# A transformer block on one core: weight slots at new SBUF distances, and another output stage

## The chip, the cores and the metric

The kernel runs on one NeuronCore of one Trainium2 chip. The metric is the device time of one execution in microseconds (us); several executions of the same program give a median. A profile is one more execution, recorded engine by engine.

The engines are named as the profile names them: PE is TensorE's matmul stream and PEld its stream of weight loads, DVE is VectorE, ACT is ScalarE, POOL is GpSimd, SP is the queue that mostly issues transfers. SBUF is the on-chip memory in front of the engines; an address in this text is a byte offset inside each of its 128 partitions. PSUM is the accumulator memory, in eight banks of 128 x 512 float32.

## What is computed

One trunk layer on x of 512 tokens x 2048 channels, float32. Cut to what matters:

```python
h = rmsnorm(x, norm_mix_pre)
y = hybrid_mixer(h, w_in, ...)          # 16 heads of forgetting attention, and an RG-LRU branch
x = x + rmsnorm(y, norm_mix_post)
h = rmsnorm(x, norm_ffn_pre)
g = causal_dwconv(h @ w_gate, conv_ffn_w, conv_ffn_b)
y = (gelu(g) * (h @ w_up)) @ w_down     # D_FF = 6144
x = x + rmsnorm(y, norm_ffn_post)       # the output
```

## The kernel before, in words

**Layout and precision.** The host lays everything out channel-major: a tile is 128 channels x 512 tokens, and there are KT = 16 tiles of x. The weights lie in DRAM in the order of use, in units of 128 x 1024 numbers (4096 bytes in each partition, eight 128 x 128 blocks of 512 bytes). Every number that enters a matmul is split into a high part (rounded by an ACT copy) and a low part (the DVE difference), and `product()` (L1475) makes three matmuls out of one: high x high, high x low, low x high. The first operand is the stationary one, loaded by a weight load, the second the moving one, streamed through. A unit is therefore 24 matmuls. SP brings a unit into `raw`, ACT writes its high half into a weight slot, DVE the low half, PE uses the slot.

**Weight slots.** Slots 0 and 1 are `w_hi[:, 0]`, `w_lo[:, 0]` and `w_hi[:, 1]`, `w_lo[:, 1]` (L143, L144). The fast products below use a third slot as well, `w_hi2`, `w_lo2` (L231, L232); `w_slot(q)` (L324) hands out slot 2, 0, 1 in turn.

**Stages.** In order of time:
1. the mixer: projections, attention, recurrence and the output projection, with the weight unit stationary (128 x 128) and the activations `act_hi`, `act_lo` moving, 512 columns wide;
2. the first six hidden tiles of gate and up (PLAIN), in the same form;
3. the other NS = 42 hidden tiles by a scheme with seven instead of eight products (L1700): `fast_product(i, n, ...)`, n from 0 to 6, each 24 matmuls with a stationary weight block and 256 moving columns of `act_hi`, `act_lo` (n = 0, 4, 5) or of the sums `tsum` (n = 1, 2, 3, 6). Product q = 7i + n uses slot 2 where q is a multiple of 3, then slot 0, then slot 1. The hidden tiles go to DRAM (`h_spill`) and come back;
4. the down projection (L1739): four groups of 24 units; here the activations are stationary and a weight slot (0 or 1) moves, 512 columns;
5. the end.

**The end.** The down projection leaves its result token-major: `y_tile(i)` for i = 0 to 3 holds 128 tokens x 2048 channels, three quarters of it in SBUF, the last quarter still in banks 4 to 7. `last_unit` (L1749) finishes one bank after the other. For each i (ACT L855, DVE L1457): ACT squares the bank (L834), DVE adds the four partial sums (L1459), ACT takes the root (L861), DVE inverts it (L1461), ACT scales the last quarter (L864) while DVE scales the first three (L1463). Then PE transposes tile after tile back to channel-major (L1785), four 128 x 128 transposes to a tile, into banks 0 to 3 in turn, in the order LIFTS. Twelve tiles (4 to 15) are finished by DVE: gain times tile plus the residual, which POOL has brought back into `x1_b` (L496, 3 MB); SP stores them in pairs (L397). Tiles 0 to 3 are finished by ACT into `y_out` (L871), and POOL sends each with a transfer that adds to what lies in the output (L499); from the third on ACT waits until the transfer before last has landed (`y_added`).

**What sets the order.** Each engine runs its own program in written order; semaphores join them. Nothing is scheduled by a planner.

**Where things lie.** Tensors are allocated in the order of the text, each start rounded up to 32 bytes. From the start of `w_hi` to the start of `act_hi` there are w_hi 8192, w_lo 8192, ones 512, eps 32, rms 2048, sq 4096, acc 2048, ident 512, cols 32, eps_y 32, y_sq 64 and y_r 64 bytes, together 25824, which is 224 modulo 512. `act_lo`, `tsum` and all their 128-column pieces lie at the same place modulo 512 as `act_hi`, and all blocks of a slot at the same place as its start. `w_hi2` lies a multiple of 512 from `act_hi`. So, modulo 512, slots 0 and 1 start 224 bytes below the activations (288 above), slot 2 at the same place. Of the small products in the mixer, `gw` against `xc`, `v` against `pt`, and `q` against `k` all lie at the same place modulo 512.

Of the kernel before, what the change touches and what calls it, by code (L numbers as in the profile page):

```python
# [24 lines left out]
F32R = mybir.dt.float32r  # L25
# [4 lines left out]
P = 128  # L30
# [28 lines left out]
ADDED = 4  # L59
LIFTS = (4, 5, 0, 6, 7, 1, 8, 9, 2, 10, 11, 3, 12, 13, 14, 15)  # L60
# [28 lines left out]
OPEN = 8  # L89
LOG1P = [1.0 / n for n in (15, 13, 11, 9, 7, 5, 3)]  # L90
# [35 lines left out]
def block_kernel(nc, xT, par_d, weights, gate_w, out):  # L126
# [3 lines left out]
    with ExitStack() as ctx:  # L130
# [6 lines left out]
        def sem(name):  # L137
# [8 lines left out]
        eps = sb("eps", [1])  # L146
# [5 lines left out]
        cols = sb("cols", [2, QT])  # L152
        eps_y = sb("eps_y", [QT])
        y_sq = sb("y_sq", [QT, GROUPS])
        y_r = sb("y_r", [3, QT])
# [3 lines left out]
        LIFT = banks[0:4]  # L159
# [71 lines left out]
        w_hi2 = sb_in(ffn, "w_hi2", [UW], F32R)  # L231
        w_lo2 = sb_in(ffn, "w_lo2", [UW], F32R)  # L232
# [10 lines left out]
        y_out = sb_in(hid, "y_out", [2, S])  # L243
        hid.close()
        fin = ExitStack()
        x1_b = sb_in(fin, "x1_b", [KT - ADDED, S])
# [16 lines left out]
            x1_back_landed lifted added taken  # L263
# [16 lines left out]
         eps_y_done, x1_back_landed, lifted, added, taken,  # L280
# [4 lines left out]
        y_added = [sem(f"y_added{s}") for s in range(2)]  # L285
# [38 lines left out]
        def w_slot(q):  # L324

            k = (q + 2) % 3
            return (w_hi2[:], w_lo2[:]) if k == 2 else (w_hi[:, k], w_lo[:, k])
# [8 lines left out]
        def _(sp):  # L336
# [168 lines left out]
        def _(act):  # L505
            def split(u, s):

                act.wait_ge(raw_landed[s], (u - s) * 8 + 16)
                at_least(act, unit_used, u - 1)
                act.activation(w_hi[:, s], raw[:, s], ACT.Copy).then_inc(hi_done, 1)  # L510

            def split_down(n, s):
# [3 lines left out]
                act.activation(w_hi[:, s], raw[:, s], ACT.Copy).then_inc(hi_done, 1)  # L516
# [310 lines left out]
            def down_square(g, i):  # L827
# [6 lines left out]
                act.activation(sq[:, 0], src, ACT.Square, accum_out=y_sq[:, i, g:g + 1]).then_inc(wdsq_done, 1)  # L834

            for g in range(GROUPS):
# [19 lines left out]
                if g < GROUPS - 1:  # L856
                    both(n + PER_GROUP, 0, 0)
            for i in range(QT):
                down_square(GROUPS - 1, i)
                act.wait_ge(y_summed, i + 1)  # L860
                act.activation(y_r[:, 1, i:i + 1], y_r[:, 0, i:i + 1], ACT.Sqrt, scale=1.0 / D,  # L861
                               bias=eps_y[:, i:i + 1]).then_inc(y_std_done, 1)
                act.wait_ge(y_r_done, i + 1)
                act.activation(y_tile(i)[:, 3 * S:], DOWN_BANKS[1][i][:], ACT.Copy, scale=y_r[:, 2, i:i + 1]).then_inc(  # L864
                    y_scaled_a, 1)
            for n, k in enumerate(LIFTS):
                if k < ADDED:
                    act.wait_ge(lifted, n + 1)
                    if k > 1:
# [977 lines left out]
```

## Time and profile before

| | us |
|---|---|
| median of 3 executions | 2336.46 (2334.82 to 2336.62) |
| the profiled execution, its own time | 2338.33 |
| span of its profile | 2336.7 |
| PE busy in it | 2281.6 (98%) |
| DVE, ACT, POOL busy | 1540.5, 996.5, 192.3 |
| granted TensorE clock, mean | 0.99 |

The span is what the trace covers; the profiled execution took 1.6 us more, and 1.9 us more than the median. In the chain of waits that ended last PE holds 94%; DVE has 2%, ACT, DMA and issue 1% each. A matmul's record is longer than its share of the time, since matmuls overlap: what one costs is the distance from its start to the next one's.

### The profile page before, as it was taken

To read this page: it belongs to the slowest core of one execution; us is meant where nothing else is said; L and a number is where in the kernel's file an instruction comes from. 1 tells how busy PE (TensorE), PEld (TensorE's weight loads), DVE (VectorE), ACT (ScalarE), POOL (GpSimd) and SP (SyncE) were. 2 spreads that over 40 slices of the span, in tenths; PEclk is the share of its full clock that TensorE was granted. 3 is DMA by queue.
4 is the path that set the end of the run, shared out by engine and by line. 5 is a ranking of instruction groups with operands and counts; after the bars stand their busy time and mean duration, and the time that the engine had idled before them with its cause. 6 is when DMAs were issued, how large, how long until landed. Compare 5 with 4: busy or idle time off the path is not lost.

```text
span 2336.7 us, 34768 instructions
## 1 busy us (share of the span) xinstructions
PE 2281.6 (98%) x13392; PEld 1998.7 (86%) x13392; DVE 1540.5 (66%) x1999; ACT 996.5 (43%) x1259; POOL 192.3 (8%) x239
## 2 busy tenths in 40 slices
PE   7999999999899899999999999999999999999996
PEld 5788888888688688999999999999998888888885
DVE  8676667667754677777777777777775444444443
ACT  5444444444422354444444444444443333343433
POOL 3000000003300000111111111111112000000000
PEclk9899999999999999999999999999999999999998
DMA  4222222222242335777777777777767332222423
GB/s 167 74 85 83 83 92 81 92 83 81 90 136 91 114 123 168 207 199 194 197 195 198 200 197 196 202 197 200 202 187 269 127 99 90 97 92 93 150 90 99
DMA packets 94246, 328.31 MB, mean 141 GB/s; under 512 B 10672, under 2 KB 14896, under 8 KB 93888
## 3 DMA queue, kind: packets, MB, share of 16 engines
q1 hardware_dynamic: 69024, 240.33, 30.0%
q0 software_dynamic: 22816, 82.36, 16.3%
q10 hardware_dynamic: 2304, 4.20, 0.5%
q8 instruction: 73, 1.20, 0.2%
q14 instruction: 29, 0.24, 0.0%
HBM read 305.83 MB, written 21.00 MB: 140 GB/s over the span
## 4 chain that ended last, share of the span: by engine, by line
PE 94%; DVE 2%; ACT 1%; issue 1%; DMA 1%; SPq 0%; POOL 0%; DVEq 0%; POOLq 0%; ACTq 0%
PE bank L1478 31%; PE bank L1479 31%; PE bank L1480 31%; PE bank L1540 1%; DVE acc_b L1142 0%; DMA x_sb<-xT 0%; ACT act_hi L636 0%; DMA out<-y_out 0%; DVE w_lo L882 0%; PE bank L1785 0%; PE bank L1508 0%; DMA h_t<-h_spill 0%; ACT w_hi L510 0%; PE bank L1559 0%; ACT act_hi L660 0%
## 5 line engine op out<-in xcount | busy, mean ns | idle before, releaser
L1478 PE MATMUL bank<-act_hi,w_hi 128*128 128x512 f32 (+1 forms) x2112 | 729.1, 345 | 22.8 <-DVE act_lo L897 14.9
L1479 PE MATMUL bank<-act_lo,w_hi 128*128 128x512 f32 (+1 forms) x2112 | 723.9, 343 | 0.0
L1480 PE MATMUL bank<-act_hi,w_lo 128*128 128x512 f32 (+1 forms) x2112 | 722.7, 342 | 0.0
L1478 PEld LDWEIGHTS bank<-act_hi,w_hi 128*128 128x128 f32 x2112 | 400.4, 190 | 80.0 <-issue 15.6
L1480 PEld LDWEIGHTS bank<-act_hi,w_lo 128*128 128x128 f32 x2112 | 400.3, 190 | 51.0
L1479 PEld LDWEIGHTS bank<-act_lo,w_hi 128*128 128x128 f32 x2112 | 400.3, 190 | 48.6 <-issue 0.5
L1479 PE MATMUL bank<-tsum,w_hi 128*128 128x256 f32 x1344 | 378.5, 282 | 0.0
L1478 PE MATMUL bank<-tsum,w_hi 128*128 128x256 f32 x1344 | 378.1, 281 | 0.0
L1480 PE MATMUL bank<-tsum,w_lo 128*128 128x256 f32 x1344 | 377.7, 281 | 0.0
L892 DVE TENSOR_TENSOR w_lo<-raw,w_hi 128x1024 fp32r<-128x1024 f32 x96 | 117.5, 1224 | 296.5 <-ACT w_hi L516 296.5
L1478 PE MATMUL bank<-w_hi,act_hi 128*128 128x512 f32 x768 | 303.5, 395 | 0.8 <-DVE w_lo L892 0.8
L1479 PE MATMUL bank<-w_lo,act_hi 128*128 128x512 f32 x768 | 303.4, 395 | 0.0
L1480 PE MATMUL bank<-w_hi,act_lo 128*128 128x512 f32 x768 | 303.4, 395 | 0.0
L882 DVE TENSOR_TENSOR w_lo<-raw,w_hi 128x1024 fp32r<-128x1024 f32 x138 | 171.9, 1245 | 197.5 <-ACT w_hi L510 194.5
L797 ACT ACTIVATE w_hi<-raw_s 128x1024 fp32r<-128x1024 f32 x168 | 178.6, 1063 | 251.3 <-PE bank L1480 248.9
L1348 DVE TENSOR_TENSOR w_lo<-raw_s,w_hi 128x1024 fp32r<-128x1024 f32 x168 | 205.8, 1225 | 82.1 <-ACT w_hi L797 82.1
L1480 PEld LDWEIGHTS bank<-tsum,w_lo 128*128 128x128 f32 x1344 | 254.4, 189 | 0.0
L1478 PEld LDWEIGHTS bank<-tsum,w_hi 128*128 128x128 f32 x1344 | 254.4, 189 | 0.0
L1479 PEld LDWEIGHTS bank<-tsum,w_hi 128*128 128x128 f32 x1344 | 254.2, 189 | 0.0
L510 ACT ACTIVATE w_hi<-raw 128x1024 fp32r<-128x1024 f32 x138 | 145.9, 1057 | 254.0 <-PE bank L1480 254.0
L516 ACT ACTIVATE w_hi<-raw 128x1024 fp32r<-128x1024 f32 x96 | 101.7, 1060 | 305.9 <-PE bank L1480 295.1
L1478 PEld LDWEIGHTS bank<-w_hi,act_hi 128*128 128x128 f32 x768 | 144.0, 187 | 36.2 <-DVE w_lo L892 1.0
(236 smaller groups left out, 2509.3 us busy)
## 6 DMA issues: line engine op xcount, KB each, us to landing
raw<-weights SPq DMA_DIRECT2D x318, 512.0 KB, 3.5
raw_s<-weights SPq DMA_DIRECT2D x84, 512.0 KB, 4.6
raw_s<-weights POOLq DMA_DIRECT2D x84, 512.0 KB, 6.1
raw_a<-weights SPq DMA_DIRECT2D x42, 512.0 KB, 4.0
h_spill<-h_out POOLq DMA_DIRECT2D x48, 256.0 KB, 3.6
h_t<-h_spill POOLq DMA_DIRECT2D x24, 512.0 KB, 6.6
x<-xT POOLq DMA_DIRECT2D x16, 256.0 KB, 3.0
out<-x ACTq DMA_DIRECT2D x16, 256.0 KB, 2.1
```

What stands on the lines that cost most here:

```text
L510: act.activation(w_hi[:, s], raw[:, s], ACT.Copy).then_inc(hi_done, 1)
L516: act.activation(w_hi[:, s], raw[:, s], ACT.Copy).then_inc(hi_done, 1)
L797: act.activation(w_slot(q)[0], RAW_OF[n](i), ACT.Copy).then_inc(hi_done, 1)
L882: dve.tensor_tensor(w_lo[:, s], raw[:, s], word(w_hi[:, s]), ALU.subtract).then_inc(split_done, 1)
L892: dve.tensor_tensor(w_lo[:, s], raw[:, s], word(w_hi[:, s]), ALU.subtract).then_inc(split_done, 1)
L1348: dve.tensor_tensor(lo, RAW_OF[n](i), word(hi), ALU.subtract).then_inc(split_done, 1)
L1478: pe.matmul(dst, ah, bh, start=start, stop=False, skip_group_check=goes_on)
L1479: pe.matmul(dst, ah, bl, start=False, stop=False, skip_group_check=goes_on)
L1480: return pe.matmul(dst, al, bh, start=False, stop=stop, skip_group_check=goes_on)
L1540: last = pe.transpose(PT[b][:, bc + P * (qt - j):bc + P * (qt - j) + P], sm[:, c:c + P], ident[:])
```

## The change

**Weight slots.** `w_0`, `w_1` and `w_2` hold high and low half of a slot one behind the other. Fillers of 64 bytes (`line_of_0`, `line_of_1`, `line_of_2`) and a new order of the tensors set where they start. Modulo 512 slot 0 now starts 64 bytes below the activations, slot 1 128 bytes below, slot 2 64 bytes above. The stream of matmuls keeps its number, order and shapes up to the last product.

**The end.** The squares are scaled by 1/D in the ACT instruction; the three earlier partial sums and the epsilon are added up by DVE before the last unit ends (`y_p`), so that the root needs only its own square. ACT takes a root of a constant ahead of them. ACT scales the last quarter of token tile i-1 after the square of tile i. All 16 channel tiles are finished by DVE in `x1_b` (now 16 tiles, read back as 4 MB, two down units later) and stored by SP one by one; `y_out`, `added`, `y_added` and POOL's adding transfers are gone. PE transposes into eight banks, and the first four channel tiles of token tiles 0 to 2 ahead of the fourth token tile.

```diff
-ADDED = 4
-LIFTS = (4, 5, 0, 6, 7, 1, 8, 9, 2, 10, 11, 3, 12, 13, 14, 15)
+LINE = 64
...
         par = sb("par", [NPAR])
+        eps = sb("eps", [1])
+        cols = sb("cols", [2, QT])
+        eps_y = sb("eps_y", [QT])
+
+        w_1 = sb("w_1", [2, UW], F32R)
+        sb("line_of_1", [LINE // 4])
+        w_0 = sb("w_0", [2, UW], F32R)
         raw = sb("raw", [2, UW])
-        w_hi = sb("w_hi", [2, UW], F32R)
-        w_lo = sb("w_lo", [2, UW], F32R)
         ones = sb("ones", [P])
...
         ident = sb("ident", [P])
+        sb("line_of_0", [LINE // 4])
+        w_hi, w_lo = (w_0[:, 0], w_1[:, 0]), (w_0[:, 1], w_1[:, 1])
...
-        w_hi2 = sb_in(ffn, "w_hi2", [UW], F32R)
-        w_lo2 = sb_in(ffn, "w_lo2", [UW], F32R)
+        sb_in(ffn, "line_of_2", [LINE // 4])
+        w_2 = sb_in(ffn, "w_2", [2, UW], F32R)
...
-            for k in range(0, KT - ADDED, 2):
-                sp.wait_ge(taken, k + 2)
-                sp.dma_start(out[:, ADDED + k:ADDED + k + 2], x1_b[:, k:k + 2]).then_inc(stored, 16)
-            sp.wait_ge(stored, 16 * (KT - ADDED) // 2)
+            for k in range(KT):
+                sp.wait_ge(taken, k + 1)
+                sp.dma_start(out[:, k], x1_b[:, k]).then_inc(stored, 16)
+            sp.wait_ge(stored, 16 * KT)
...
-            pool.wait_ge(h_split, 3 * PER_GROUP + 6)
-            pool.dma_start(x1_b[:], out[:, ADDED:KT]).then_inc(x1_back_landed, 16)
-            for k in range(ADDED):
-                pool.wait_ge(added, k + 1)
-                pool.dma_start(out[:, k], y_out[:, k % 2], accum_op=ALU.add).then_inc(y_added[k % 2], 16)
-            for e in range(2):
-                pool.wait_ge(y_added[e], 16 * ADDED // 2)
+            pool.wait_ge(h_split, (GROUPS - 1) * PER_GROUP + KT // 2)
+            pool.dma_start(x1_b[:], out).then_inc(x1_back_landed, 16)
...
+            act.activation(y_s[:, 0:1], eps[:, 0:1], ACT.Sqrt).then_inc(y_std_done, 1)
+            act.wait_ge(y_std_done, 1)
+            act.wait_ge(y_summed, 3)
             for i in range(QT):
                 down_square(GROUPS - 1, i)
+                if i:
+                    scale_last(i - 1)
+                token_root(i)
+            scale_last(QT - 1)
...
+            dve.tensor_tensor(y_p[:, 0], y_sq[:, 0], y_sq[:, 1], ALU.add).then_inc(y_summed, 1)
+            dve.tensor_tensor(y_p[:, 1], y_sq[:, 2], eps_y[:], ALU.add).then_inc(y_summed, 1)
+            dve.wait_ge(y_summed, 2)
+            dve.tensor_tensor(y_p[:, 0], y_p[:, 0], y_p[:, 1], ALU.add).then_inc(y_summed, 1)
...
+            for k in range(KT):
+                dve.wait_ge(lifted, k + 1)
+                dve.scalar_tensor_tensor(out=x1_b[:, k], in0=banks[k % 8][:], scalar=col("g_ffn_post", k),
+                                         in1=x1_b[:, k], op0=ALU.mult, op1=ALU.add).then_inc(taken, 1)
...
+            for i in range(QT - 1):
+                pe.wait_ge(y_scaled_d, i + 1)
+                for k in range(4):
+                    lift(k, i)
+            pe.wait_ge(y_scaled_d, QT)
+            for k in range(4):
+                lift(k, QT - 1).then_inc(lifted, 1)
+            pe.wait_ge(y_scaled_a, QT)
+            for k in range(4, KT):
+                at_least(pe, taken, k - 7)
                 for i in range(QT):
-                    if n == 0:
-                        pe.wait_ge(y_scaled_d, i + 1)
-                    last = pe.transpose(LIFT[n % 4][:, P * i:P * i + P], y_tile(i)[:, P * k:P * k + P], ident[:])
+                    last = lift(k, i)
                 last.then_inc(lifted, 1)
```

How the change moves instructions is shown at two places. The first is ACT's program from the last split of activations on (`sq` the scratch of the squares, `y_r`, `y_s` root and inverse, `y_a`, `y_b` the token tiles). Before:

```order
L524 ACTIVATE act_hi<-h_t 128x4x256 [waits unit_used]
L834 ACTIVATE sq,y_sq<-bank4 128x512 [waits last_done]
L861 ACT_TABLE_LOAD
L861 ACTIVATE y_r<-y_r,eps_y 128x1 [waits y_summed]
L864 ACTIVATE y_a<-bank4,y_r 128x512 [waits y_r_done]
L834 ACTIVATE sq,y_sq<-bank5 128x512 [waits last_done]
L861 ACTIVATE y_r<-y_r,eps_y 128x1 [waits y_summed]
L864 ACTIVATE y_a<-bank5,y_r 128x512 [waits y_r_done]
```

and in the changed kernel:

```order
L522 ACTIVATE act_hi<-h_t 128x4x256 [waits unit_used]
L868 ACT_TABLE_LOAD
L868 ACTIVATE y_s<-eps 128x1
L832 ACTIVATE sq,y_sq<-bank4 128x512 [waits last_done,y_summed,y_std_done]
L865 ACTIVATE y_s<-y_sq,y_p 128x1 [waits wdsq_done]
L832 ACTIVATE sq,y_sq<-bank5 128x512 [waits last_done]
L859 ACTIVATE y_a<-bank4,y_r 128x512 [waits y_r_done]
L865 ACTIVATE y_s<-y_sq,y_p 128x1 [waits wdsq_done]
L832 ACTIVATE sq,y_sq<-bank6 128x512 [waits last_done]
```

The table load has moved ahead of the first square of the last group, the root waits for ACT's own square only, and each scaling stands behind the next square.

The second is PE's program behind the last product: the transposes. Before, from the first to the one that waits for a freed bank:

```order
L1785 MATMUL bank0<-ident,y_a 128x128 [waits y_scaled_d] x2
L1785 MATMUL bank0<-ident,y_b 128x128 [waits y_scaled_d] x2
L1785 MATMUL bank1<-ident,y_a 128x128 x2
L1785 MATMUL bank1<-ident,y_b 128x128 x2
L1785 MATMUL bank2<-ident,y_a 128x128 x2
L1785 MATMUL bank2<-ident,y_b 128x128 x2
L1785 MATMUL bank3<-ident,y_a 128x128 x2
L1785 MATMUL bank3<-ident,y_b 128x128 x2
L1785 MATMUL bank0<-ident,y_a 128x128 [waits taken]
```

and in the changed kernel, the fourth token tile's and what follows:

```order
L1784 MATMUL bank0<-ident,y_b 128x128 [waits y_scaled_d]
L1784 MATMUL bank1<-ident,y_b 128x128
L1784 MATMUL bank2<-ident,y_b 128x128
L1784 MATMUL bank3<-ident,y_b 128x128
L1784 MATMUL bank4<-ident,y_a 128x128 [waits y_scaled_a]
L1784 MATMUL bank4<-ident,y_a 128x128
L1784 MATMUL bank4<-ident,y_b 128x128 x2
L1784 MATMUL bank5<-ident,y_a 128x128 x2
L1784 MATMUL bank5<-ident,y_b 128x128 x2
```

Twelve transposes now stand before the first row of this piece, three to each of banks 0 to 3, so that one more completes a tile; the first wait for a freed bank comes with the ninth tile instead of the fifth, and no wait for `added` is left.

## Rows read from the trace of the kernel before

**Rows 1.** The page: span, and section 1 (busy us, share, instructions).
```profile
span 2336.7 us, 34768 instructions
PE 2281.6 (98%) x13392; PEld 1998.7 (86%) x13392; DVE 1540.5 (66%) x1999; ACT 996.5 (43%) x1259; POOL 192.3 (8%) x239
```

**Rows 2.** Groups of PE by form: line, names, shape, xcount | busy us, mean ns | idle before.
```profile
L1478 PE MATMUL bank<-act_hi,w_hi 128*128 128x512 f32 x1104 | 445.6, 404 | 22.8 <-DVE act_lo L897 14.9 <-DVE act_lo L1159 7.0 <-DVE w_lo L882 0.9
L1478 PE MATMUL bank<-tsum,w_hi 128*128 128x256 f32 x1344 | 378.1, 281 | 0.0
L1478 PE MATMUL bank<-w_hi,act_hi 128*128 128x512 f32 x768 | 303.5, 395 | 0.8 <-DVE w_lo L892 0.8
L1478 PE MATMUL bank<-act_hi,w_hi 128*128 128x256 f32 x1008 | 283.5, 281 | 0.0
```

**Rows 3.** Timeline of PE, rounds 18 to 20: start us, us; first matmuls of products 0 and 1.
```profile
1291.22 0.28 PE L1478 MATMUL bank<-act_hi,w_hi 128*128 128x256 f32 x1
...
1294.09 0.28 PE L1478 MATMUL bank<-tsum,w_hi 128*128 128x256 f32 x1
...
1311.17 0.28 PE L1478 MATMUL bank<-act_hi,w_hi 128*128 128x256 f32 x1
...
1314.00 0.28 PE L1478 MATMUL bank<-tsum,w_hi 128*128 128x256 f32 x1
...
1331.08 0.28 PE L1478 MATMUL bank<-act_hi,w_hi 128*128 128x256 f32 x1
...
1333.92 0.28 PE L1478 MATMUL bank<-tsum,w_hi 128*128 128x256 f32 x1
```

**Rows 4.** Timeline of PE, down projection: two matmuls that stand 24 apart.
```profile
2289.97 0.40 PE L1478 MATMUL bank<-w_hi,act_hi 128*128 128x512 f32 x1
...
2295.57 0.40 PE L1478 MATMUL bank<-w_hi,act_hi 128*128 128x512 f32 x1
```

**Rows 5.** Timeline of PE, gate product of the mixer: the first and sixth of six.
```profile
308.92 0.40 PE L1478 MATMUL bank<-xc_hi,gw_hi 128*128 128x512 f32 x1
...
310.06 0.39 PE L1480 MATMUL bank<-xc_hi,gw_lo 128*128 128x512 f32 x1
```

**Rows 6.** Timeline of PE, attention scores: two matmuls that stand two apart.
```profile
364.24 0.40 PE L1479 MATMUL bank<-k_lo,q_hi 64*128 64x512 f32 x1
...
364.71 0.34 PE L1478 MATMUL bank<-k_hi,q_hi 64*128 64x384 f32 x1
```

**Rows 7.** Timeline of the end, ACT and DVE, with the idle time before and its releaser.
```profile
2304.17 0.60 ACT L834 ACTIVATE sq<-bank 128x512 f32<-128x512 f32 x1 [4.93 <-PE bank L1480]
...
2306.17 0.29 ACT L861 ACTIVATE y_r<-y_r,eps_y 128x1 f32<-128x1 f32 x1
...
2312.22 0.29 ACT L861 ACTIVATE y_r<-y_r,eps_y 128x1 f32<-128x1 f32 x1 [0.23 <-DVE y_r L1459]
...
2312.75 1.02 DVE L1463 TENSOR_SCALAR y_b<-y_b,y_r 128x1536 f32<-128x1536 f32 x1
...
2314.40 1.54 DVE L1469 SCALAR_TENSOR_TENSOR x_b<-bank,par,x_b 128x512 f32<-128x512 f32 x2 [0.64 <-PE bank L1785]
...
2316.89 4.29 DVE L1469 SCALAR_TENSOR_TENSOR x_b<-bank,par,x_b 128x512 f32<-128x512 f32 x6 [0.95 <-PE bank L1785]
...
2326.88 0.75 DVE L1469 SCALAR_TENSOR_TENSOR x_b<-bank,par,x_b 128x512 f32<-128x512 f32 x1 [2.00 <-PE bank L1785]
```

**Rows 8.** DMA issues: line, engine, xcount, KB each, us to landing.
```profile
out<-x_b SPq DMA_DIRECT2D x1, 512.0 KB, 5.0
...
out<-x ACTq DMA_DIRECT2D x16, 256.0 KB, 2.1
```

**Rows 9.** SP's queue: the last store.
```profile
2327.66 0.33 SPq L397 DMA_DIRECT2D out<-x_b  x1
```

**Rows 10.** ACT while the residual comes back; one stretch's busy us, PEclk, DMA share, GB/s.
```profile
2213.96 1.06 ACT L516 ACTIVATE w_hi<-raw 128x1024 fp32r<-128x1024 f32 x1 [4.38 <-DMA raw<-weights]
...
2205.00:2210.00 5.00, 5.00 (x23) 4.00 (x22) 1.76 (x3) 2.01 (x2) 0.00 (x0) 1.00 0.98 409
```

More of the change, by code:

```diff
@@ L262, in block_kernel @@
             wd_taken wdsq_done y_summed y_std_done y_r_done y_scaled_a y_scaled_d diag_done spread_done eps_y_done
-            x1_back_landed lifted added taken
+            x1_back_landed lifted taken
             stored dve_chain""".split()
@@ L279, in block_kernel @@
          wd_taken, wdsq_done, y_summed, y_std_done, y_r_done, y_scaled_a, y_scaled_d, diag_done, spread_done,
-         eps_y_done, x1_back_landed, lifted, added, taken,
+         eps_y_done, x1_back_landed, lifted, taken,
          stored, dve_chain) = [sem(n) for n in names]
@@ L857, in _, with scale_last, token_root @@
                     both(n + PER_GROUP, 0, 0)
+            def scale_last(i):
+                act.wait_ge(y_r_done, i + 1)
+                act.activation(y_tile(i)[:, 3 * S:], DOWN_BANKS[1][i][:], ACT.Copy, scale=y_r[:, i:i + 1]).then_inc(
+                    y_scaled_a, 1)
+            def token_root(i):
+                n = QT * (GROUPS - 1) + i + 1
+                act.wait_ge(wdsq_done, n)
+                act.activation(y_s[:, i:i + 1], y_sq[:, GROUPS - 1, i:i + 1], ACT.Sqrt, bias=y_p[:, 0, i:i + 1]).then_inc(
+                    y_std_done, 1)
+            act.activation(y_s[:, 0:1], eps[:, 0:1], ACT.Sqrt).then_inc(y_std_done, 1)
+            act.wait_ge(y_std_done, 1)
+            act.wait_ge(y_summed, 3)
             for i in range(QT):
                 down_square(GROUPS - 1, i)
[L860 to L869, printed above, removed]
[L870 to L872 removed]
+                if i:
+                    scale_last(i - 1)
+                token_root(i)
+            scale_last(QT - 1)
         @block.vector
@@ L1745, in down_unit @@
                         last = product(bank[:], (h_tokens(act_hi, s, kt, i), h_tokens(act_lo, s, kt, i)),
-                                       (w_hi[:, s, w], w_lo[:, s, w]), start and kt == 0, stop and kt == 1)
+                                       (w_hi[s][:, w], w_lo[s][:, w]), start and kt == 0, stop and kt == 1)
                 last.then_inc(unit_used, 1)
@@ L1774, in _, with lift @@
                     last_unit(n + PER_GROUP - 1, 1, out_banks)
-            for n, k in enumerate(LIFTS):
-                if n >= 4:
-                    before = LIFTS[:n - 3]
-                    at_least(pe, taken, sum(b >= ADDED for b in before))
-                    at_least(pe, added, sum(b < ADDED for b in before))
-                if k == 12:
-                    pe.wait_ge(y_scaled_a, QT)
+            def lift(k, i):
+                return pe.transpose(banks[k % 8][:, P * i:P * i + P], y_tile(i)[:, P * k:P * k + P], ident[:])
+            for i in range(QT - 1):
[8 more added lines that the diff above has]
+                at_least(pe, taken, k - 7)
                 for i in range(QT):
-                    if n == 0:
-                        pe.wait_ge(y_scaled_d, i + 1)
-                    last = pe.transpose(LIFT[n % 4][:, P * i:P * i + P], y_tile(i)[:, P * k:P * k + P], ident[:])
+                    last = lift(k, i)
                 last.then_inc(lifted, 1)
```

50 lines of the change are left out of this document (20 added, 30 removed).

## The prediction

> **What bounds the kernel now.** I read the page first: PE is busy for 98% of the span [rows 1]. Only two things can move the time: the distance from one matmul's start to the next, or the end, where PE no longer sets the pace. The groups by form [rows 2] give the counts. There are three times 1104 and three times 768 matmuls of 512 columns, together 5616, and three times 1344 and three times 1008 of 256 columns, together 7056; the latter are 294 products of 24. The idle time before them is about 24 us in all, most of it before the first form. So the timeline is needed for their distances.
>
> *256 columns.* One product 0 stands alone between the tsum products, so its length can be read [rows 3]. It is 1294.09 - 1291.22 = 2.87 us in slot 2, 2.83 in slot 0 (round 19) and 2.84 in slot 1 (round 20). I looked at all 42 rounds: it is the same each time, to 0.01 us. Per matmul that is 119.6, 117.9 and 118.3 ns. Slot 2 is the one that starts at the activations' own place modulo 512 bytes; the other two start 288 above.
>
> *512 columns.* In the down projection 24 matmuls take 5.60 us, 233.3 ns each [rows 4], at slots 0 and 1 alike, and the earlier stages, with the roles of the operands exchanged, run at the same. The small gate product, whose operands lie at the same place modulo 512, has five distances in 1.14 us, 228 ns each [rows 5]. The score product, also at the same place but on 64 partitions, has two in 0.47 us, 235 ns [rows 6]. So the trace shows that the place of a slot can matter, by one or two per cent, and not always in the same direction.
>
> *The end* [rows 7]. From the first square (2304.17) ACT and DVE go in turn: the first root comes at 2306.17, two microseconds later, and three rounds of 2.02 us each follow until 2312.22. DVE scales the last token tile from 2312.75 to 2313.77, the first channel tile is taken from 2314.40, and the last, after gaps, ends at 2327.63. The store issued at 2327.66 [rows 9] takes 5.0 us to land [rows 8], to 2332.66; another 4.0 us end the span.
>
> **The change, part by part.**
>
> *The token rounds.* The first root no longer waits for a table load and DVE's sum: it can start when the square ends, at 2304.17 + 0.69 + 0.02 = 2304.88 (the square of 0.60 and its read of the sum occupied ACT for 0.69). Round 0's DVE scaling starts 0.53 after its root, as at the end before (2312.22 to 2312.75). A round on ACT is now square 0.69, scaling 0.58 and root with handover 0.33, 1.60 us in place of 2.02, since DVE's handovers lie beside the next square. The second square has to wait for its bank, which is ready six matmuls after the first, at 2304.17 + 6 x 0.2333 = 2305.57. The roots then come at 2304.88, 2306.88, 2308.49 and 2310.10. DVE's last scaling runs from 2310.63 to 2311.65, against 2313.77: **2.1 us earlier**. The table load moves into ACT's idle 4.93 us; the three small DVE sums end before the first square too, and if that cover were gone they would cost a few tenths.
>
> *The tiles.* DVE's first tile starts 0.63 after its last scaling, as before, at 2312.28. Six tiles in a row take 4.29 us, 0.715 each; sixteen take 11.44 and end at 2323.72. Before, twelve tiles ended at 2327.63 because DVE stood waiting for banks that ACT held while it waited for its adding transfers. PE has three quarters of four tiles ready and a lead of eight banks, so I cost its transposes at nothing; if the cover went, the next in line is PE's cold clock. **In sum 3.9 us earlier** than before (the 2.1 are in it).
>
> *The stores.* Sixteen of 256 KB in 11.44 us ask for 367 GB/s; with the residual coming back the engines moved 409 [rows 10]. The last store before had 512 KB and an adding transfer beside it and took 5.0; a plain one of 256 KB took 2.1 [rows 8]. I take 2.8, nearer to the latter, because the demand stays below 409. It lands at 2326.6, and 4.0 more give 2330.6: **6.1 us less**, between 3.9 (landing as before) and 6.8.
>
> *The residual* comes back as 4 MB. While 3 MB did, one load of weights came late enough for ACT to wait 4.38 us for it [rows 10], and yet all down units together cost PE 0.8 us of idle [rows 2]. I take nothing; the bound is 2.6 us, the time of the added megabyte at 409 GB/s. POOL's queue holds nothing else behind it.
>
> *Slot 2* moves from distance 0 to 64. Among the 98 products in it each is 0.035 us longer than the mean of the other two slots; if it runs like them, 98 x 0.035 = **3.4 us less**. The other end is nothing, and a gain.
>
> *Slots 0 and 1 at 256 columns* have 196 products. From nothing to the pace of slot 2, 98 x 0.04 + 98 x 0.03 = 6.9 us more. I take nothing: their distances are new, but none of them is 0.
>
> *512 columns.* No row has the new distances of -64 and -128. The bounds are the gate product, 5616 x 5.3 ns = 29.8 us less, and the score product, 5616 x 1.7 ns = 9.5 us more. Slot 0 at -64 is nearest to distance 0, where the two small products disagree in sign; slot 1 at -128 is nearer to the present place. I take nothing, with a chance for the gain below.
>
> The sum is -6.1 - 3.4 = -9.5. The profiled execution would go from 2338.3 to 2328.8, its span to 2327.2; against the median of 2336.46 I forecast **2327.0**.
>
> One rule speaks against the first half of the change. What the rows show is the 2.87 against 2.83 us [rows 3]. The Trainium skill (TensorE: Matmul & The Clock Gate, "Step-by-step: what each phase is for") has PE read its moving operand and its weights through two independent ports, so that loading the next weights takes nothing from the running matmul; by it the slots' places would be worth nothing. This trace disagrees for slot 2, if the place is what sets it apart. The same page ("Back-to-back issue gap") gives N/2.4 + 2.5 ns, as an estimate 216 ns for 512 columns, so that 17 ns of the 233 here would have some other cause; were all of that a clash of two reads and all of it gone, the gain would be near 100 us, which no row supports.
>
> **The rivals.**
>
> *The 512-column matmuls get faster.* For it speaks the gate product at 228 ns [rows 5], in every one of its occurrences; against it the score product. In full the time is 2336.5 - 6.1 - 3.4 - 29.8 = 2297.2. If by nearest row only slot 0's half gains (2808 x 5.3 = 14.9) and its 256-column products pay 3.9, it is 2336.5 - 6.1 - 14.9 + 3.9 = 2319.4.
>
> *The places do nothing.* Slot 2 is longer for another reason than its place, such as its low half lying 4096 bytes behind its high half (8192 in the other slots), and stays so. Then only the end counts: 2336.5 - 6.1 = 2330.4. The rule above says that much too.
>
> *The new places are worse.* Two streams a line apart could meet more often than two far apart; and all three slots now have the 4096 bytes of slot 2. At the pace of slot 2 everywhere and of the score product at 512 columns it costs 6.9 + 9.5 = 16.4, and the time is 2346.8; at half of that, 2338.6. It ends above the present time as soon as the places cost more than the 6.1 us of the end, 1.1 ns for each 512-column matmul or 0.9 ns for each one of 256.
>
> *The transfers bound the end.* Stores one by one run behind DVE and land as late as before, and the fourth megabyte costs PE 1 us: 2336.5 - 3.9 - 3.4 + 1.0 = 2330.2. For it speaks that 367 is close to 409.
>
> **How the numbers follow.** A difference of 0.2% is 4.7 us, about what a measurement of this kernel can tell from no change. My chances are 0.42 for the forecast, 0.25 for faster 512-column matmuls, 0.13 for places that do nothing, 0.12 for worse places and 0.08 for the transfers. The range goes from 2299, which leaves out only the last part of the full gain, to 2338, where worse places cost half; past either end some 2 in 10 stay out. The forecast's own range is 2324 to 2330. Faster by over 0.2%: nearly all of the first (0.41), all of the second (0.25), most of the third and of the last (0.12), 0.78. Slower by over 0.2% takes most of the worse places, 0.11. The rest, 0.11, is within 0.2%.
>
> **What would show it.** In the changed profile product 0 should take 2.83 to 2.84 us in slot 2 as well; 24 matmuls of the down projection should still take 5.60 us, and about 5.47 if the first rival is right; the first root should come 0.7 us after the first square; sixteen tiles should take 11.4 us without a gap on DVE; and the last store should land within 3 us. The forecast is wrong if those 5.60 us change by more than 0.01, either way, since 0.01 us is worth 2.3 us of the kernel, or if DVE waits for PE between tiles.

## The result, and the profile after

The changed kernel takes 2295.27 us (median of 4 executions, 2293.55 to 2299.04) against 2336.54 for the kernel before (4 executions, 2334.82 to 2338.06): a ratio of 0.9826, with a 95% interval of 0.9809 to 0.9843. That is 41 us less, where 9.5 were forecast, and below the end of the range (2299). The profiled execution has a span of 2293.1 us against 2336.7 [rows 1]:

```profile
span 2293.1 us, 34762 instructions
...
PE 2248.9 (98%) x13392; PEld 1975.0 (86%) x13392; DVE 1543.0 (67%) x2002; ACT 993.7 (43%) x1256; POOL 188.5 (8%) x235
```

PE has the same 13392 matmuls and is again busy for 98%, yet its busy time is 33 us shorter. So most of the gain lies in how closely the matmuls follow each other, and the stages show where. In the timeline of PE I take the first matmul of the fast products, the first of the down projection and the last product. Before:

```profile
932.55 0.28 PE L1478 MATMUL bank<-act_hi,w_hi 128*128 128x256 f32 x1
...
1770.46 0.50 PE L1478 MATMUL bank<-w_hi,act_hi 128*128 128x512 f32 x1 [0.84 <-DVE w_lo L892]
...
2307.94 0.40 PE L1480 MATMUL bank<-w_hi,act_lo 128*128 128x512 f32 x1
```

and after:

```profile
925.43 0.28 PE L1485 MATMUL bank<-act_hi,w 128*128 128x256 f32 x1
...
1739.92 0.50 PE L1485 MATMUL bank<-w,act_hi 128*128 128x512 f32 x1 [0.94 <-DVE w L896]
...
2275.98 0.40 PE L1487 MATMUL bank<-w,act_lo 128*128 128x512 f32 x1
```

| us | before | after | gain |
|---|---|---|---|
| up to the first fast product (512 columns, slot stationary) | 932.6 | 925.4 | 7.1 |
| fast products (256 columns) | 837.9 | 814.5 | 23.4 |
| down projection (512 columns, slot moving) | 537.5 | 536.1 | 1.4 |
| from the last product's start to the end of the span | 28.8 | 17.1 | 11.6 |

The four gains are those of one profiled execution on each side and add up to 43.6 us, the difference of the two spans; the medians differ by 41.3. The first stage is the least certain one: another kernel with the same places (the second of the next section) reaches the fast products at 923.1 us, not 925.4.

The rows that answer to those of product 0 [rows 3], rounds 18 to 20, slots 2, 0 and 1:

```profile
1274.02 0.28 PE L1485 MATMUL bank<-act_hi,w 128*128 128x256 f32 x1
...
1276.76 0.28 PE L1485 MATMUL bank<-tsum,w 128*128 128x256 f32 x1
...
1293.36 0.28 PE L1485 MATMUL bank<-act_hi,w 128*128 128x256 f32 x1
...
1296.08 0.28 PE L1485 MATMUL bank<-tsum,w 128*128 128x256 f32 x1
...
1312.68 0.28 PE L1485 MATMUL bank<-act_hi,w 128*128 128x256 f32 x1
...
1315.52 0.28 PE L1485 MATMUL bank<-tsum,w 128*128 128x256 f32 x1
```

Slot 2 (now at +64) takes 2.74 us instead of 2.87, slot 0 (-64) 2.72 instead of 2.83, slot 1 (-128) 2.84 as before.

The end, in the timeline of ACT, DVE and SP, answering to [rows 7]:

```profile
2272.31 0.60 ACT L832 ACTIVATE sq<-bank 128x512 f32<-128x512 f32 x1 [3.49 <-PE bank L1487]
...
2273.03 0.29 ACT L865 ACTIVATE y_s<-y_sq,y_p 128x1 f32<-128x1 f32 x1
...
2277.57 0.29 ACT L865 ACTIVATE y_s<-y_sq,y_p 128x1 f32<-128x1 f32 x1
...
2278.09 1.02 DVE L1471 TENSOR_SCALAR y_b<-y_b,y_r 128x1536 f32<-128x1536 f32 x1
...
2279.60 10.63 DVE L1476 SCALAR_TENSOR_TENSOR x_b<-bank,par,x_b 128x512 f32<-128x512 f32 x16 [0.49 <-PE bank L1784]
...
2280.38 10.21 SPq L400 DMA_DIRECT2D out<-x_b  x16
```

The first root comes 0.72 us after the first square; DVE's last scaling ends 6.8 us after that square (9.6 before); sixteen tiles run without a gap, 0.66 us each; and the last store, issued at 2290.26 and landing 2.5 us later, ends the span but for 0.4 us. In SP's queue the wait behind the last landing has all but gone. Before:

```profile
SPq L130 <- DMA out<-x_b: 4.7, 1, 4.7
SPq L130 <- PEq L130: 3.8, 1, 3.8
```

and after (engine, line, waited for: us in total, times, longest):

```profile
SPq L129 <- DMA out<-x_b: 2.1, 1, 2.1
SPq L129 <- PEq L129: 0.2, 1, 0.2
```

### The profile page after: what moved, and what is told of

The parts are those of the page before. It is cut to its first block, busy times and chain, and to the rows that moved or that the text cites. A ratio compares the mean times of both kernels' runs of the same rounds, so it can differ in the third digit from the quotient of the medians.

```text
span 2293.1 us, 34762 instructions
## 1 busy us (share of the span) xinstructions
PE 2248.9 (98%) x13392; PEld 1975.0 (86%) x13392; DVE 1543.0 (67%) x2002; ACT 993.7 (43%) x1256; POOL 188.5 (8%) x235
## 3 DMA queue, kind: packets, MB, share of 16 engines
q10 hardware_dynamic: 2304, 4.20, 0.5%
## 4 chain that ended last, share of the span: by engine, by line
PE 94%; DVE 3%; issue 1%; ACT 1%; DMA 0%; POOL 0%; SPq 0%; DVEq 0%; POOLq 0%; ACTq 0%
PE bank L1485 31%; PE bank L1486 31%; PE bank L1487 31%; PE bank L1547 1%; DVE x_b L1476 0%; DVE acc_b L1146 0%; DMA x_sb<-xT 0%; DVE act_lo L901 0%; PE bank L1515 0%; DVE w L886 0%; DMA h_t<-h_spill 0%; ACT act_hi L658 0%; ACT w L508 0%; ACT x_sb L642 0%; PE bank L1566 0%
## 5 line engine op out<-in xcount | busy, mean ns | idle before, releaser
L1485 PE MATMUL bank<-act_hi,w 128*128 128x512 f32 (+1 forms) x2112 | 722.4, 342 | 21.5 <-DVE act_lo L901 14.9
L1486 PE MATMUL bank<-act_lo,w 128*128 128x512 f32 (+1 forms) x2112 | 717.5, 340 | 0.0
L1487 PE MATMUL bank<-act_hi,w 128*128 128x512 f32 (+1 forms) x2112 | 717.4, 340 | 0.0
L1485 PEld LDWEIGHTS bank<-act_hi,w 128*128 128x128 f32 x2112 | 398.8, 189 | 76.8 <-issue 16.1
L1487 PEld LDWEIGHTS bank<-act_hi,w 128*128 128x128 f32 x2112 | 398.8, 189 | 47.8
L1486 PEld LDWEIGHTS bank<-act_lo,w 128*128 128x128 f32 x2112 | 398.8, 189 | 46.9 <-issue 0.5
L1486 PE MATMUL bank<-tsum,w 128*128 128x256 f32 x1344 | 374.0, 278 | 0.0
L1485 PE MATMUL bank<-tsum,w 128*128 128x256 f32 x1344 | 373.4, 278 | 0.0
L1487 PE MATMUL bank<-tsum,w 128*128 128x256 f32 x1344 | 373.3, 278 | 0.0
L896 DVE TENSOR_TENSOR w<-raw,w 128x1024 fp32r<-128x1024 f32 x96 | 117.7, 1226 | 295.1 <-ACT w L514 295.0
L1485 PE MATMUL bank<-w,act_hi 128*128 128x512 f32 x768 | 303.0, 395 | 1.0 <-DVE w L896 0.9
L1487 PE MATMUL bank<-w,act_lo 128*128 128x512 f32 x768 | 303.0, 395 | 0.0
L1486 PE MATMUL bank<-w,act_hi 128*128 128x512 f32 x768 | 302.8, 394 | 0.0
L886 DVE TENSOR_TENSOR w<-raw,w 128x1024 fp32r<-128x1024 f32 x138 | 171.9, 1246 | 190.7 <-ACT w L508 188.0
L1487 PEld LDWEIGHTS bank<-tsum,w 128*128 128x128 f32 x1344 | 252.7, 188 | 0.0
L1485 PEld LDWEIGHTS bank<-tsum,w 128*128 128x128 f32 x1344 | 252.6, 188 | 0.0
L508 ACT ACTIVATE w<-raw 128x1024 fp32r<-128x1024 f32 x138 | 145.7, 1057 | 246.6 <-PE bank L1487 241.2
L1486 PEld LDWEIGHTS bank<-tsum,w 128*128 128x128 f32 x1344 | 252.4, 188 | 0.0
L514 ACT ACTIVATE w<-raw 128x1024 fp32r<-128x1024 f32 x96 | 101.7, 1059 | 304.5 <-PE bank L1487 292.6
```

The costliest lines, as they stand in the source:

```text
L508: act.activation(w_hi[s], raw[:, s], ACT.Copy).then_inc(hi_done, 1)
L514: act.activation(w_hi[s], raw[:, s], ACT.Copy).then_inc(hi_done, 1)
L886: dve.tensor_tensor(w_lo[s], raw[:, s], word(w_hi[s]), ALU.subtract).then_inc(split_done, 1)
L896: dve.tensor_tensor(w_lo[s], raw[:, s], word(w_hi[s]), ALU.subtract).then_inc(split_done, 1)
L1485: pe.matmul(dst, ah, bh, start=start, stop=False, skip_group_check=goes_on)
L1486: pe.matmul(dst, ah, bl, start=False, stop=False, skip_group_check=goes_on)
```

## The experiments

Distances below are from the activations to a slot's start, modulo 512 bytes; the change has slots 0, 1 and 2 at -64, -128 and +64, the kernel before at -224, -224 and 0. Where a kernel has one profile and one time only, it is read by its stages: 0.01 us in one product of 24 matmuls is 2.9 us over the 294 fast products.

**The two halves apart.** The first kernel has the new end and the old places, the second the old end and the new places. The diff is the first one's, against the changed kernel.

```diff
-        w_1 = sb("w_1", [2, UW], F32R)
-        sb("line_of_1", [LINE // 4])
-        w_0 = sb("w_0", [2, UW], F32R)
         raw = sb("raw", [2, UW])
+        w_his = sb("w_his", [2, UW], F32R)
+        w_los = sb("w_los", [2, UW], F32R)
...
-        sb("line_of_0", [LINE // 4])
+        sb("as_far_as_before", [56])
...
-        sb_in(ffn, "line_of_2", [LINE // 4])
```

> The changed kernel with the slots where they were before (slots 0 and 1 at -224 from the activations modulo 512 bytes, slot 2 at 0, halves 8192 bytes apart in slots 0 and 1). Theory (the places and the end are two separate gains): the 42 rounds of fast products take 838 us again, as before the change, and from the first square of the last group to the end of the span it takes 20.8 us as in the changed kernel, not 32.5: 2336.5 - 11.7 = 2324.8. Rival (the end was helped by the earlier stages, for instance by transfers that stand otherwise): the end keeps well over 20.8 us.

> The kernel before with the slots at their new places and nothing else. Theory: 2336.5 - 31.9 = 2304.6, of which some 23.4 us in the fast products; product 0 takes 2.72, 2.84 and 2.74 us in slots 0, 1 and 2. Rival (some of it is due to the end's new tensors): less than 28 us of gain.

The end alone: 2327.35 us against 2337.28, ratio 0.9954 (0.9938 to 0.9971). The fast products take 837.8 us as before, and the last product's start stands 17.1 us from the end of the span. The places alone: 2306.36, ratio 0.9868 (0.9852 to 0.9885); fast products 814.5, end 28.6. The gains, 9.9 and 30.9 us, add up to the whole 41.3. So each half works by itself, and neither borrows from the other, as far as these intervals (some 4 us either way) can tell.

**Slot 1 at -64 too.**

```diff
         w_1 = sb("w_1", [2, UW], F32R)
-        sb("line_of_1", [LINE // 4])
         w_0 = sb("w_0", [2, UW], F32R)
```

> The changed kernel with slot 1 too at -64 instead of -128. Theory (what counts is a slot's own distance to the activations): product 0 takes 2.72 us in slot 1 instead of 2.84; 98 products by 0.12 us are 11.8 us, so 2283.5. Rival (the slots have to differ from each other, since ACT and DVE write one while PE reads another): slot 0 loses what it had gained, and the time is 2295 or more.

2277.45 us, ratio to the kernel before 0.9744 (0.9728 to 0.9760): 18 us faster than the change. The timeline of PE, product 0 in slot 0 and in slot 1, then the first down matmul:

```profile
1281.95 0.28 PE L1484 MATMUL bank<-act_hi,w 128*128 128x256 f32 x1
...
1284.67 0.28 PE L1484 MATMUL bank<-tsum,w 128*128 128x256 f32 x1
...
1300.99 0.28 PE L1484 MATMUL bank<-act_hi,w 128*128 128x256 f32 x1
...
1303.71 0.28 PE L1484 MATMUL bank<-tsum,w 128*128 128x256 f32 x1
...
1721.17 0.50 PE L1484 MATMUL bank<-w,act_hi 128*128 128x512 f32 x1 [1.14 <-DVE w L895]
```

All three slots now take 2.72 us, 113.3 ns for a matmul; the 42 rounds take 801.0 us, 13.5 less than in the change; and the stages before them end 5.3 us earlier, at 920.2 (one profile each; the change's places gave 925.4 and 923.1). "Each at its own distance" is thus no help in itself: three slots at the same 64 bytes do better. The 11.8 us I expected left out that slot 2's products drop from 2.74 to 2.72 with a faster neighbour, and the 512-column stages. Slot 1 lies at the same address in this kernel, in the next one and in the whole sweep below; only the activations move against it. Its products take between 2.72 and 2.88 us there, so its own address is not what sets its pace.

**The halves of a slot together, at the old distances.**

```diff
-        sb("line_of_1", [LINE // 4])
...
-        sb("line_of_0", [LINE // 4])
+        sb("line_of_0", [56])
...
-        sb_in(ffn, "line_of_2", [LINE // 4])
```

> The changed kernel with slots 0 and 1 at -224 and slot 2 at 0, as before the change, but with the halves of each slot one behind the other (4096 bytes), as the change has them. Theory (distance to the activations): 2.83, 2.84 and 2.87 us for product 0 in slots 0, 1, 2 as before the change, about 2325. Rival (it is the distance between the halves that counts): slots 0 and 1 change by 0.03 us or more.

2327.31 us (one time), fast products 837.8 us, product 0 at 2.84, 2.84 and 2.86 us. The distance between a slot's halves, which the change altered too, is not the cause.

**A sweep of the distance.** Only the fillers' sizes change: slots 0 and 1 both at one distance, slot 2 at another. In words of four bytes the first filler is 8, 24, 32 and 48 and left out in the last kernel, the second 24, 40, 8, 48 and 16; the diff shows the first of the five.

```diff
-        sb("line_of_1", [LINE // 4])
...
-        sb("line_of_0", [LINE // 4])
+        sb("line_of_0", [8])
...
-        sb_in(ffn, "line_of_2", [LINE // 4])
+        sb_in(ffn, "line_of_2", [24])
```

> The changed kernel with slots 0 and 1 at -32 and slot 2 at +96. Known so far for a 256-column product: 2.72 us at -64 and +64, 2.84 at -128 and -224, 2.87 at 0. Theory (a window around 64 bytes on either side is good, the exact value does not matter): 2.72 to 2.78 us at both. Rival (only whole 64-byte lines are good, 32 and 96 straddle): 2.84 or more at both, 2325 in all.

> The changed kernel with slots 0 and 1 at -96 and slot 2 at +160. Theory (window around 64): -96 between 2.72 and 2.84, +160 at 2.84. Rival (lines): both 2.84.

> The changed kernel with slots 0 and 1 at -128 and slot 2 at +32. Theory (each slot by its own distance): slots 0 and 1 take 2.84 us, so that the 42 rounds take 838 us less what slot 2 gains at +32, and 24 matmuls of the down projection less than 5.60, near 5.57, since slot 1 at -128 must be what made that stage 1.4 us shorter in the changed kernel (slot 0 at -64 shows 5.60 alone). Rival (slots have to differ): the down projection is as before.

> The changed kernel with slots 0 and 1 at -192 and slot 2 at +192. Of the distances so far, those that agree modulo 256 gave the same pace (-96 and +160: 120.0 ns; -224 and +32: 118.3 and 118.1). Theory (256 bytes are the period): -192 and +192 are +64 and -64 modulo 256, 2.72 us for every product and 801 us for the 42 rounds. Rival (512 is the period, only the nearest lines are good): 2.84 or more.

> The changed kernel with slots 0 and 1 at the activations' own place (0), slot 2 at +64. At 256 columns both theories expect 2.86 us in slots 0 and 1. At 512 columns: if the gate product of the mixer (228 ns, operands at the same place) tells what a slot at 0 does, the time up to the first fast product is 918 us or less and 24 matmuls of the down projection take 5.47 us. Rival (a short product of six matmuls does not tell it): 5.60 us and 930 us.

The stages in us, from the same three points of PE's timeline, with those kernels that have slots 0 and 1 at one distance (42 rounds and down projection in us):

| slots 0 and 1 | slot 2 | to the first fast product | product 0 in slot 0 | 42 rounds | down projection | single time |
|---|---|---|---|---|---|---|
| -224 (new end, halves together) | 0 | 933.0 | 2.84 | 837.8 | 537.6 | 2327.31 |
| -192 | +192 | 933.6 | 2.72 | 801.1 | 527.9 | 2280.97 |
| -128 | +32 | 930.0 | 2.84 | 836.6 | 538.1 | 2323.51 |
| -96 | +160 | 931.2 | 2.88 | 847.6 | 541.1 | 2338.57 |
| -64 | +64 | 920.2 | 2.72 | 801.0 | 537.5 | 2277.44 |
| -32 | +96 | 932.6 | 2.80 | 826.3 | 538.5 | 2316.13 |
| 0 | +64 | 913.4 | 2.88 | 842.3 | 522.7 | 2297.24 |

The last row's points in the timeline of PE are:

```profile
913.40 0.28 PE L1483 MATMUL bank<-act_hi,w 128*128 128x256 f32 x1
...
1755.74 0.50 PE L1483 MATMUL bank<-w,act_hi 128*128 128x512 f32 x1 [0.70 <-DVE w L894]
...
2278.43 0.39 PE L1485 MATMUL bank<-w,act_lo 128*128 128x512 f32 x1
```

Three things follow. *At 256 columns* 64 bytes are best, on either side, and so are 192: of the distances tried, those that agree modulo 256 agree in pace (-192 is +64, and -96 is +160), so the period is 256 bytes, not 512. The neighbouring -96 is the slowest of all, 120.0 ns a matmul, slower than anything in the kernel before, so neither the window around 64 of my first theory nor its rival, under which -32 should have been no better than 2.84 us, holds. *At 512 columns* 0 is best by far, and the first rival's row was right: the down projection takes 226.9 ns for a matmul at 0, where the gate product [rows 5] had shown 228; -192 shows 229 and the other distances 233 to 235. *The sign counts there*: a slot at -64 gains where it is stationary (920.2) and not where it moves (537.5); a slot at -192, that is +64, gains where it moves (527.9) and not where it is stationary (933.6). Both say that at 512 columns the stationary block should start at the moving operand's place or 64 bytes below it.

The third kernel's expectation missed on the down projection: -128 alone does not shorten it. That the change's mixture of -64 and -128 does, by 1.4 us, is not explained; in the change's trace the units of slot 1 take 5.58 us on the mean and those of slot 0 5.60, so it is slot 1 that gains beside a neighbour at -64.

A slot's own distance is thus not the whole story. At 256 columns slot 2 at +64 takes 2.83 us between two slots at 0, and 2.72 between two at -64. And the gate product of the mixer [rows 5], whose two operands keep their distance in every kernel here, takes 1.14 us from its first to its sixth matmul in seven of eight occurrences before, and 1.16 in six of eight after the change:

```profile
306.39 0.40 PE L1485 MATMUL bank<-xc_hi,gw_hi 128*128 128x512 f32 x1
...
307.55 0.39 PE L1487 MATMUL bank<-xc_hi,gw_lo 128*128 128x512 f32 x1
```

Over all layouts it lies between 1.135 and 1.161 us, 227 to 232 ns a matmul, with nothing changed between its own operands. What else in a layout acts on it was not tried.

The denser stream can be read off stretches of equal length as well. For the kernel with slots at 0, from 1900 us on (columns: stretch, its length, busy us and instructions of PE, PEld, DVE, ACT, POOL, then PEclk, DMA share, GB/s):

```profile
1900.00:2000.00 100.00, 100.00 (x442) 82.78 (x442) 44.73 (x39) 37.66 (x40) 0.00 (x0) 1.00 0.30 97
```

and for the kernel before the same stretch and one of the fast products:

```profile
1100.00:1300.00 200.00, 200.00 (x1689) 200.00 (x1688) 157.19 (x192) 89.38 (x100) 23.45 (x30) 1.00 0.74 198
1900.00:2000.00 100.00, 100.00 (x430) 80.31 (x430) 44.90 (x40) 38.67 (x44) 0.00 (x0) 1.00 0.28 94
```

442 matmuls stand where 430 did, at the same granted clock of 1.00, and PE's busy time is 100.00 of 100.00 in both. A full busy share therefore says nothing of the pace. (The first of the two rows is a stretch of fast products: 1689 matmuls in 200 us, 118.4 ns each.)

**Slots 0 and 1 on either side.**

```diff
-        par = sb("par", [NPAR])
         eps = sb("eps", [1])
...
         w_1 = sb("w_1", [2, UW], F32R)
-        sb("line_of_1", [LINE // 4])
+        par = sb("par", [NPAR])
+        sb("line_of_1", [8])
         w_0 = sb("w_0", [2, UW], F32R)
```

> The changed kernel with slot 1 at +64 instead of -128, slots 0 and 2 as in the change (-64 and +64). Theory (each slot by its own distance, +64 and -64 alike): 800 us for the 42 rounds as with all slots 64 away, 2277.5 in all. If two differing slots have something to themselves at 512 columns (in the changed kernel, with -64 and -128, the down projection was 1.4 us shorter than with either distance alone), the down projection takes 536 instead of 537.5 here too. Rival (+64 is worse for a slot that also serves the 512-column stages): the time up to the first fast product is over 925 us.

2281.10 us, ratio 0.9759 (0.9743 to 0.9776), 3.6 us above the theory. The 42 rounds take 801.0 us, as the theory has it, but at 512 columns the rival on record was right, and the down projection is not at the 536 that a gain of differing slots would give. There slot 1 at +64 behaves as the sweep says: 927.3 us to the first fast product, halfway between 920.2 and 933.6, and 532.5 us of down projection, halfway between 537.5 and 527.9.

**The end of the end.** The last store goes to POOL's queue (on top of slot 1 at -64), and in a second kernel it also adds to the output, (`accum_op=ALU.add`, not in the diff), which puts the residual of the last tile in twice.

```diff
-            for k in range(KT):
+            for k in range(KT - 1):
                 sp.wait_ge(taken, k + 1)
                 sp.dma_start(out[:, k], x1_b[:, k]).then_inc(stored, 16)
-            sp.wait_ge(stored, 16 * KT)
+            sp.wait_ge(stored, 16 * (KT - 1))
+            sp.wait_ge(x1_back_landed, 32)
...
             pool.dma_start(x1_b[:], out).then_inc(x1_back_landed, 16)
+            pool.wait_ge(taken, KT)
+            pool.wait_ge(x1_back_landed, 16)
+            pool.dma_start(out[:, KT - 1], x1_b[:, KT - 1]).then_inc(x1_back_landed, 16)
```

> The kernel with slot 1 at -64, and the last of the 16 stores issued by POOL instead of SP. In the kernel before, 4.0 us passed from the landing of the last transfers to the end of the span, in the changed kernel 0.4. Theory (a transfer of POOL's queue near the end makes the end 3 to 4 us longer): about 3.6 us are back, span 2279.5, beside 1 us for a longer landing. Rival (the 3.6 us came with the adding transfers or with waiting engines, not with POOL's queue): the span grows by at most 1.5 us over 2275.8.

> As the run with the last store issued by POOL (which ended the span 2.1 us later than SP's stores did: 19.2 us from the last product's start to the end, against 17.2), but the last transfer adds to what lies in the output, as the kernel before had it; the last tile's residual is so added twice. Theory (adding transfers are what makes the end long): 2 us or more on top, 21 us from the last product to the end. Rival (POOL's queue alone costs the 2.1, and adding only its own longer landing): within 1 us of 19.2.

From the last product to the end it takes 19.2 us with POOL's plain store and 21.2 with the adding one, against 17.2. What SP waited for at the end, of the first and of the second kernel:

```profile
SPq L401 <- DMA out<-x_b: 3.0, 1, 3.0
SPq L129 <- PEq L129: 2.1, 1, 2.1
```

```profile
SPq L401 <- DMA out<-x_b: 4.9, 1, 4.9
SPq L129 <- PEq L129: 2.1, 1, 2.1
```

One transfer of POOL's queue at the very end makes the wait behind the last landing 2.1 us instead of 0.2; adding leaves that wait alone and makes the landing 1.9 us later (3.0 to 4.9). The span of the first grew by 1.4 us, inside what the rival allowed, but only since its first stages were 0.8 us shorter; its end grew by 2.1. So the theory's 3 to 4 us from POOL's queue did not come. One such transfer accounts for 1.9 of the 3.6 us by which the wait was shorter in the change.

What SP waits for there is not PE, whose name the row has: POOL's last instruction, a DRAIN, ends 0.23 us before the span in both kernels and in the kernel before. The packed traces hold it, though no view of the profile lists it. In the two kernels above it starts as POOL issues its last transfer and ends 2.09 us after that has landed. In the kernel before POOL waits for its adding transfers first; the DRAIN starts at 2332.73, with all landed, and takes 3.70 us. In the changed kernel it ends at 2195.88, long before the end. That points to POOL's own wait, and not to the adding, for the remaining 1.7 us; no kernel with that wait and a plain transfer was tried.

**Each stage at its own best distance.** Slots 0 and 1 get 64 bytes more, and are used from two starts: 64 bytes below the activations in the fast products, at the activations' own place elsewhere.

```diff
-        par = sb("par", [NPAR])
-        eps = sb("eps", [1])
...
-        w_1 = sb("w_1", [2, UW], F32R)
-        sb("line_of_1", [LINE // 4])
-        w_0 = sb("w_0", [2, UW], F32R)
+        w_1 = sb("w_1", [2 * UW + LINE // 4], F32R)
+        par = sb("par", [NPAR])
+        eps = sb("eps", [1])
+        cols = sb("cols", [2, QT])
+        eps_y = sb("eps_y", [QT])
+        w_0 = sb("w_0", [2 * UW + LINE // 4], F32R)
...
+        def halves_at(w, c):
+            return w[:, c:c + UW], w[:, c + UW:c + 2 * UW]
+
+        w_hi, w_lo = zip(halves_at(w_0, LINE // 4), halves_at(w_1, LINE // 4))
...
-            return (w_2[:, 0], w_2[:, 1]) if k == 2 else (w_hi[k], w_lo[k])
+            return (w_2[:, 0], w_2[:, 1]) if k == 2 else halves_at((w_0, w_1)[k], 0)
```

> The changed kernel with slots 0 and 1 used from two starts: 64 bytes below the activations in the fast products (256 columns), at the activations' own place (0) in all stages of 512 columns; slot 2 stays at +64. Theory (what a matmul costs hangs on the distance between the block being loaded and the moving operand modulo 256, and on the width: at 256 columns 64 is best and 0 worst, at 512 columns 0 is best): 913.4 us to the first fast product and 522.7 us of down projection as with slots at 0, 801 us for the 42 rounds as with all at 64, 17.1 us of end; the span 2255.7, the time 2257. Rival (the two gains came from the kernels' other differences and do not add up): 2270 or more.

2257.46 us against 2337.81, ratio 0.9655 (0.9642 to 0.9668): 38 us faster than the change, 80 faster than the kernel before, and within 0.5 us of the 2257 on record. (The four stages named there add up to a span of 2254.2 us, not 2255.7; the profiled execution has 2256.7, 2.5 more.) Its points in PE's timeline are the first fast product, product 0 of round 19, the first down matmul and the last product:

```profile
914.66 0.28 PE L1485 MATMUL bank<-act_hi,w 128*128 128x256 f32 x1
...
1276.74 0.28 PE L1485 MATMUL bank<-act_hi,w 128*128 128x256 f32 x1
...
1279.46 0.28 PE L1485 MATMUL bank<-tsum,w 128*128 128x256 f32 x1
...
1715.96 0.50 PE L1485 MATMUL bank<-w,act_hi 128*128 128x512 f32 x1 [1.14 <-DVE w L896]
...
2239.53 0.39 PE L1487 MATMUL bank<-w,act_lo 128*128 128x512 f32 x1
```

914.7, 801.3, 523.6 and 17.2 us: the gains of both distances are in one kernel, which reads the same slots at one distance in one stage and at the other in the next. So it is the distance, and the width with it, that carries these gains, and not some other trait of the two layouts.

## Why the prediction was wrong

**What held.** That only the matmuls' distances and the end could move the time; that the two halves of the change are separate; slot 1 at 256 columns (2.84 us, unchanged); DVE without gaps over sixteen tiles; the residual's fourth megabyte at nothing (the down projection did not get longer); the first root 0.7 us after its square. The sign was right.

**The step that failed: "Slots 0 and 1 at 256 columns ... I take nothing", and slot 2's 3.4 us.** I bounded both by the two paces that the trace showed, 118 and 119.6 ns, and let the better one be the best there is: "if it runs like them". The new distances gave a third, 113.3 to 114.2 ns, outside those bounds: 23.4 us in place of 3.4. The trace held no row below 118 ns for 256 columns, so its own rows could not bound the gain. What it did show was that the place matters at all; from there the lower end should have been left open as far as, by an estimate, the stream's own length, 107 ns for 256 columns if one goes in per cycle at the granted 2.4 GHz (the 1.00 in the rows).

**"512 columns ... I take nothing."** The two stages gained 7.1 and 1.4 us. The rival's row, the gate product at 228 ns, pointed the right way: slots at distance 0 give 227 ns. I discounted it because the score product at the same distance read 235; that product runs on 64 partitions, and it should have counted for less than the one of the same form. But six matmuls were weak evidence: it was not 228 ns "in every one of its occurrences" (one of eight took 1.16 us), and in the change's own trace most of them read 232, so that the agreement with 227 is in part luck. The change's own distances use only a part of that gain: slot 0 at -64, and only where it is stationary.

**The end: 11.6 us in place of 6.1.** By its terms, from the first square on. The token rounds gave 2.8 for 2.1: I summed ACT's three instructions to 1.60 us a round, but their records overlap, and the last roots follow each other in 1.40 us, which is also the pace at which the banks come. The tiles gave 2.7 for 1.8, since sixteen in a row take 0.66 us each, not 0.715. The last store gave 2.6 for 2.2, landing in 2.5 us where I took 2.8. And 3.6 came from a term that I had copied over unchanged, the 4.0 us between the last landing and the end of the span; with POOL's transfers, and the DRAIN behind them, out of the end it is 0.4. This was the larger part of the miss at the end: a term carried over without a reason. The down projection's sign of being wrong, "if those 5.60 us change by more than 0.01", came in slot 1 (5.58).

**The rule.** That weight loads and the moving operand use two ports and take nothing from each other (the Trainium skill, TensorE: Matmul & The Clock Gate, "Step-by-step: what each phase is for") does not fit the sweep: the same matmuls cost between 113.3 and 120.0 ns, and between 227 and 235, as the place of one operand against the other changes. No run here takes the weight loads away, so that it is these two reads that meet is likely, not shown. As an estimate the same page's N/2.4 + 2.5 ns ("Back-to-back issue gap"), which it gives for an isolated matmul, comes to 109 and 216 ns; the best distances found here come within 4 and 11 ns of it. The same section's figure for pairs of weight load and matmul, about 131 ns at 512 columns, is far below all that these traces show.

## What to carry to other kernels

When PE is busy for 98% of the span, read its pace from start to start and set it against the columns at the granted clock; if a few per cent are missing, move the stationary tensor by 64 bytes against the moving one and look again, for each width that the kernel uses, since the best place at one width can be nearly the worst at another (distance 0: 227 ns at 512 columns, 120 at 256). A bound taken from the paces that a trace happens to show is a bound of nothing when the change makes a new case. And terms "as before" at the very end of a kernel need a cause, too: look for which engine or queue is waited for.

## What the runs showed that I had not expected

- The cost of a matmul on fp32r operands depends on the distance modulo 256 bytes between stationary and moving operand: 113.3 ns (64, 192), 116.6 (-32), 118.3 (-128, -224), 120.0 (0, -96) at 256 columns with slots 0 and 1 at one distance. The neighbouring slots' distance matters as well (113.3 or 118 ns for slot 2 at +64).
- At 512 columns it is 227 ns at 0, 229 in the down projection where the stationary operand starts 64 bytes below the moving one modulo 256 (527.9 us for 2304 matmuls), and 233 to 235 at the other distances of that stage. The sign counts at this width; at 256 columns -64 and +64 do the same.
- PE's busy share and the granted clock (1.00) show nothing of this; only the number of matmuls in a stretch does (430 or 442 in 100 us).
- A single transfer of POOL's queue at the end of the kernel costs 2 us behind its own landing, in which POOL's DRAIN still runs; behind four that POOL had waited for, the DRAIN took 3.7 us.
- Which mechanism in the chip makes the two reads cost each other time stays open; the runs show the distances, the widths and the period only.
